# Odd attention: both heads' turned probabilities copied by one ScalarE operation, VectorE's copy removed

## The reference, cut to what matters

```python
def safe_softmax(s, mask):
    ...
    e = jnp.exp(s - m)
    den = jnp.sum(e, axis=-1, keepdims=True)
    return e / jnp.where(den > 0, den, 1.0)

def nsa_mixer(q, kc_raw, vc_raw, ks, vs, kw, vw, gates, pe, w1, w2, pos):
    ...
        p_cmp = safe_softmax(s, (cmp_end[None, :] <= t[:, None])[:, None, None, :])
        o_cmp = jnp.einsum('bqghn,bngd->bqghd', p_cmp.astype(v_cmp.dtype), v_cmp)
        ...
        o_slc = jnp.einsum('bqghnl,bgqnld->bqghd', p.astype(vg.dtype), vg)
        ...
        o_win = jnp.einsum('bqghs,bsgd->bqghd', p.astype(vwb.dtype), vwb)
        g = qslice(gates, i, C_Q_BLOCK)
        return g[..., 0:1] * o_cmp + g[..., 1:2] * o_slc + g[..., 2:3] * o_win
```

## Time and profile before

| | us |
|---|---|
| median of three runs | 1133.84 |
| the profiled execution, whole | 1134.03 |
| its span | 1132.3 |
| PE busy | 998.5 |
| DVE busy | 590.4 |
| ACT busy | 486.2 |
| POOL busy | 101.8 |

### The profile page before, as it was taken

One profiled execution on the slowest core, in us unless ns is written; L12 is line 12 of the kernel. 1 busy time (PEld: TensorE's weight loads), 2 busy tenths in 40 slices (PEclk: granted clock), 3 DMA queues, 4 the chain that ended last, 5 costly groups with the idle time before them and its releaser, 6 DMA issues. The chain is left out here.

```text
span 1132.3 us, 20170 instructions
## 1 busy us (share of the span) xinstructions
PE 998.5 (88%) x8499; PEld 713.1 (63%) x8499; DVE 590.4 (52%) x950; ACT 486.2 (43%) x795; POOL 101.8 (9%) x111
## 2 busy tenths in 40 slices
PE   6998899889666677998889999997998879999996
PEld 5676787445333344886537777775985546777773
DVE  5666678431000004688675554536666865655543
ACT  5455463310000004554556455524545656645532
POOL 3410270000000001034000000002040000000000
PEclk9998799889888899998889999998998999999998
DMA  8823004999999996452094755534421056666520
GB/s 275 253 82 120 2 3 173 424 408 419 420 421 421 421 413 215 150 181 80 1 312 136 250 184 184 197 111 147 155 82 75 1 186 205 223 222 207 186 88 37
DMA packets 108324, 228.56 MB, mean 202 GB/s; under 512 B 7145, under 2 KB 86043, under 8 KB 93659
## 3 DMA queue, kind: packets, MB, share of 16 engines
q1 hardware_dynamic: 105275, 219.38, 53.3%
q0 software_dynamic: 2976, 8.14, 2.4%
HBM read 224.63 MB, written 1.05 MB: 199 GB/s over the span
## 5 line engine op out<-in xcount | busy, mean ns | idle before, releaser
L524 DVE SCALAR_TENSOR_TENSOR ffn_wu_lo<-ffn_w_up,ffn_wu_hi 128x2048 f16<-128x2048 f32 x44 | 99.0, 2288 | 55.2 <-ACT ffn_wu_hi L449 55.2
L1132 PE MATMUL rw_pB<-ring,kept 128*32 128x256 f32 x864 | 72.6, 434 | 26.9 <-DMA ring<-in_w_up 22.5
L669 PE MATMUL ffn_pG<-ffn_hT_hi,ffn_wu_hi 128*128 128x256 f16 x352 | 95.9, 273 | 0.3
L669 PE MATMUL ffn_pU<-ffn_hT_hi,ffn_wu_hi 128*128 128x256 f16 x352 | 96.0, 273 | 0.0
L669 PE MATMUL ffn_pU<-ffn_hT_lo,ffn_wu_hi 128*128 128x256 f16 x352 | 96.0, 273 | 0.0
L669 PE MATMUL ffn_pU<-ffn_hT_hi,ffn_wu_lo 128*128 128x256 f16 x352 | 96.0, 273 | 0.0
L669 PE MATMUL ffn_pG<-ffn_hT_hi,ffn_wu_lo 128*128 128x256 f16 x352 | 95.9, 273 | 0.0
L669 PE MATMUL ffn_pG<-ffn_hT_lo,ffn_wu_hi 128*128 128x256 f16 x352 | 95.9, 273 | 0.0
L449 ACT ACTIVATE ffn_wu_hi<-ffn_w_up 128x2048 f16<-128x2048 f32 x44 | 81.7, 1901 | 2.4 <-DMA ffn_w_up<-in_ffn_w_gate 2.3
L1132 PEld LDWEIGHTS rw_pB<-ring,kept 128*32 128x32 f32 x864 | 39.1, 125 | 53.4 <-issue 40.7
L1065 DVE TENSOR_TENSOR rw_mu_a<-rw_pB,rw_mu_a 128x256 f32<-128x256 f32 x8 | 3.4, 425 | 130.6 <-PE rw_pB L1132 130.6
(11 more groups left out here) (655 smaller groups left out, 2141.0 us busy)
## 6 DMA issues: line engine op xcount, KB each, us to landing
ring<-in_w_gate SPq DMA_DIRECT2D x27, 1024.0 KB, 26.4
ring<-in_w_up SPq DMA_DIRECT2D x27, 1024.0 KB, 26.5
ring<-in_w_down SPq DMA_DIRECT2D x24, 1024.0 KB, 26.3
ffn_w_up<-in_ffn_w_gate SPq DMA_DIRECT2D x22, 1024.0 KB, 7.7
ffn_w_up<-in_ffn_w_up SPq DMA_DIRECT2D x22, 1024.0 KB, 9.9
ffn_w_down<-in_ffn_w_down SPq DMA_DIRECT2D x22, 1024.0 KB, 5.1
wt<-in_ev_w_in SPq DMA_DIRECT2D x9, 1024.0 KB, 5.6
wt<-in_od_w_in SPq DMA_DIRECT2D x9, 1024.0 KB, 5.5
```

Of the source, the lines that this page charges most:

```text
L524: return nc.vector.scalar_tensor_tensor(out, whole, scale, hi, ALU.mult, ALU.subtract)
L669: ins = T.matmul(p[:, s, j * SEQ:(j + 1) * SEQ], w[:, s, m, c, j::NJ], h[:, c, :], start=(n == 0), stop=(n == 3 * KC - 1))
L1132: ins = nc.tensor.matmul(into[i * CAP:(i + 1) * CAP, 0:D_EXPERT], h[:, c, i * CAP:(i + 1) * CAP], held[:, c * D_EXPERT:(c + 1) * D_EXPERT] ...
```

## The change

ScalarE's `right(u)` becomes `copy_turned(u)`, at the same place of its order: it copies both banks of `pT` (2 times 384 columns) to both heads' part of `ET` in one operation. VectorE's `left(u)` goes. One semaphore, `probs_copied`, takes the place of `probs_left` and `probs_right`; TensorE waits for it where it waited for both. The even layer's attention, which has such copies of its own, stays as it is.

```diff
@@ ScalarE
-                    def right(u):
+                    def copy_turned(u):
                         act.wait_ge(probs_turned, u + 1)
                         if u >= 2:
                             act.wait_ge(summed, u - 1)
-                        nc.scalar.activation(ET[:, u % 2, 1, :], pT[:, 1, 0:NCOL], ACT.Copy).then_inc(probs_right, 1)
+                        nc.scalar.activation(ET[:, u % 2, :, :], pT[:, :, 0:NCOL], ACT.Copy).then_inc(probs_copied, 1)
...
-                        right(u)
+                        copy_turned(u)
@@ VectorE
-                    def left(u):
-                        dve.wait_ge(probs_turned, u + 1)
-                        if u >= 2:
-                            dve.wait_ge(summed, u - 1)
-                        nc.vector.tensor_copy(ET[:, u % 2, 0, :], pT[:, 0, 0:NCOL]).then_inc(probs_left, 1)
...
-                        left(u)
@@ TensorE, turn(u)
-                            pe.wait_ge(probs_left, u)
-                            pe.wait_ge(probs_right, u)
+                            pe.wait_ge(probs_copied, u)
@@ TensorE, add_values(u)
-                        pe.wait_ge(probs_left, u + 1)
-                        pe.wait_ge(probs_right, u + 1)
+                        pe.wait_ge(probs_copied, u + 1)
```

More of the change, by code:

```diff
@@ L3454, in sparse_attention @@
         with Stage(nc, "nsa", ["scored", "least", "exped", "weighed", "probs_turned",
-                               "probs_left", "probs_right", "summed", "high_out", "low_out", "c_scored", "c_masked",
+                               "probs_copied", "summed", "high_out", "low_out", "c_scored", "c_masked",
                                "c_less", "c_exped", "c_weighed", "c_turned", "c_out", "gate_exps", "vlink"]) as sems:
-            (scored, least, exped, weighed, probs_turned, probs_left, probs_right, summed,
+            (scored, least, exped, weighed, probs_turned, probs_copied, summed,
              high_out, low_out, c_scored, c_masked, c_less, c_exped, c_weighed, c_turned, c_out, gate_exps, vlink) = sems
```

## The result

The changed kernel takes 1137.65 us (median of 20 runs, 1131.99 to 1141.64), the kernel before 1133.88 in the 20 runs beside it (1127.4 to 1139.32): ratio 1.0031, 95% interval 1.0016 to 1.0046, so 1.8 to 5.2 us slower. Two later series of 12 runs gave 1.0023 (0.9992 to 1.0053) and 1.0041 (1.0017 to 1.0065). The ratios compare undisturbed executions only and need not equal the quotient of the medians. The forecast was 1137.0, a ratio of 1.0026 to the profiled execution of before.

A forecast was written before the change was run, and what follows sets the result against it. The attention's pace, set by a loop once through ScalarE and over TensorE (6.89 us per two units), was to pass to one through ScalarE twice (7.26). 0.45 + 1.90 + 0.31 + 0.36 = +3.0 on 1134.0: 1137.0 us, range 1134.8 to 1139.4.

The forecast's parts named there:

- The ScalarE copy: ScalarE's 16 copies grow from 384 to 768 columns, 0.808 us against 0.504, so +0.31 us each.
- The rings: Steady attention: the loop through ScalarE twice, 6.64 us, becomes 7.26 and sets the pace of two units.
- ring B: Steady attention: loop once through ScalarE, then over TensorE; sets today's pace, 6.89 us per two units, and becomes 7.20.
- The start: From the attention's first copies through the compressed scores to exps(5): +0.45 us.
- copy(13): Attention's tail: this copy makes turn(14) 0.31 us later still.
- The last values: Attention's end: copy(15) runs 0.81 us, TensorE follows 0.16 behind its end; +0.36 us.
- VectorE as the bound: Rival, odd steps: VectorE's copy delays its minimum, so removing it gains 3.3 us, 1130.7; chance 0.05.
- all hidden: Rival: ScalarE's 16.2 us of waits in the attention swallow the longer copies, 1134.0; chance 0.06.
- The dearer copy: Rival: +0.50 us a copy on some 14 copies on the path, +2.8 on top, 1139.8; chance 0.08.
- Ring B alone: Rival: turn does not hold exps in the steady attention, two units in 7.20 us, total 1136.7; chance 0.14.
- The clock: Rival behind the attention: TensorE's clock falls once more or not at all, 1138.7 or 1135.3; chance 0.07 each way.
- Two of the signs: Expected in the profile: exps named as waiting for turn, and the attention ending near 921.0 instead of 917.95.

The follow-up runs named there:

- three halves of E: Changed kernel with three halves of buffer E instead of two, so exps(u + 2) waits for turn(u - 1); one execution took 1136.57 us.
- the kernel with two: Changed kernel with ScalarE's one copy of 768 columns made as two of 384; one execution took 1134.94 us.
- filler: Changed kernel with ten products more on TensorE ahead of turn(14), scores computed again and never read; ratio 1.0023 (0.9999 to 1.0047).
- two copies ahead of exps: Kernel before, one copy on each engine, with ScalarE's copy moved ahead of exps(u + 2); ratios 0.9972 and 0.9979.

## Why the prediction was right, step by step

The time, 1137.65, lies in the range, and the sum, 3.0 us, in the interval of 1.8 to 5.2. That the median comes within 0.7 of 1137.0 is in part luck: two terms were sized too high, and the clock, which the sum left out, added to it where it fell, in two profiles of three. By its own steps:

- The shift of the block behind the attention: right. From the first issue of the next stage to the end of the span it is 213.46 us before and 213.43 after.
- VectorE's copy worth nothing in the steady stretch: right (6.88 with and without it). VectorE's subtraction starts 0.42 behind the high copy, as forecast (880.84 to 881.26).
- The ScalarE copy: 0.82 us in place, against 0.81 taken from the other stage's row, which has the same shape but is a Relu with a scale; whether that makes the difference was not tried. By the rule of the Trainium skill ("ScalarE: Activation LUTs", section "What ACT_TABLE_LOAD costs") it would have been 0.826; the 16 copies' mean is 0.824, so here the trace agrees with the page more closely than with the row I used.
- The rings: right. 7.26 was forecast, 7.27 measured, in all three profiles of the changed kernel; ring B at 7.20 is shown by three halves of E. The five periods from exps(5) to exps(15) went from 34.41 to 36.35 (871.97 to 908.32): +1.94, forecast +1.90.
- The start: mis-sized. copy(0) put turn(1) 0.31 later, in the sum and in the trace (copy to turn is 0.65 before, 0.96 after); from there to exps(5) the sum had +0.14 more (0.45 in all), and the trace has 0.11 less, so 0.20 in all. I took 0.81 from turn(2) to the transposes, a step from values behind turn, where they follow in 0.68; and of the 1.53 behind them 0.15 went, where I had allowed 0.03. Before, VectorE's copy L3578 had to stand behind its minimum L3513 and started 0.80 behind the transposes (870.97); now it starts 0.64 behind them (867.64). The kernel without VectorE's copy gives this term alone: 0.43 less from turn(1) to turn(3). With the 0.32 that copy(1) puts on turn(2) it makes the 0.11 less of the trace.
- copy(13): +0.31, forecast 0.31.
- The last values: mis-sized a little. In the second profile of the changed kernel, at the full clock, turn(15) to L3628 is 2.47 us (920.97 to 923.44), before 2.23: +0.24 instead of +0.36. The weights of the last eight products load 0.05 behind the copy's end, where I had 0.16 to PE.

Together 0.20 + 1.94 + 0.31 + 0.24 = +2.7 us of the change's own, 0.24%. The three series give 0.31, 0.23 and 0.41%, all with intervals that hold it. If the clock's fall came in the tail in two of three executions, as in the profiles, it would add 0.9 and the sum would be 3.6; that is an estimate from three profiles and not shown.

The rivals: VectorE as the bound and all hidden are excluded by the profile of the kernel without its copy and by 7.27. The dearer copy is excluded by 0.82 us for the copy and by 7.27, and a dearer one has its own number, 7.39, in the kernel with two; its price in the prediction was added wrongly, as 14 times 0.19 is 2.7 and not 2.8. Ring B alone is excluded by 7.27 against 7.20.

The clock is the rival that I priced in the wrong place. Its case was a fall more or less at the start of the next stage. There the fall came before and after alike (0.50 from 922 to 924 us in both), and that stretch is equally long. The fall that the change was followed by lay in the tail of the attention, in two profiles of three, where I had argued against it with the wait of 2.02 us, and it cost 1.3 instead of 1.7. A chance of 0.07 was small for that, though three profiles don't tell how often it comes. If in addition the low level at the start belonged to the changed kernel, the sum would be 2.7 + 3.1 = 5.8, an estimate that lies above the first interval.

Two of the signs did not show. Exps was not named as waiting for turn; that turn held it is shown by the distance of 0.08 and by three halves of E. And the attention's end cannot be held against 921.0: the next stage's first issue came at 919.57, 0.7 later than before and not 3.0, because the stage had begun 6.6 earlier.

## What to carry to other kernels

Close the rings before you price a merged operation: an engine with idle time can still be the one whose every microsecond counts, if its operation stands between two of the busiest engine. Two engines' copies side by side cost 0.50 where one engine's double copy costs 0.82, so here merging them lost while the copy stood on the ring and, by the profiles alone, gained once the order had taken it off. And look at the order first: putting the operation that frees the next step ahead of the long one that does not left the kernel some 5 us under the kernel before with one copy (and so some 8 under the changed kernel) and some 3 with two, and with it the one copy looks the better, where without it it was the worse.

## What the runs showed that I had not expected

- The name of a wait for two engines can be wrong: exps was put down to VectorE's minimum in each period, before and after. In every other step of the changed kernel that minimum had ended 0.40 us before exps, and turn 0.08 before; and cutting turn's link changed the pace. Compare the ends of all that an instruction waits for.
- TensorE's clock can fall inside a stage: behind a wait of 2.12 us (2.19 with two copies on ScalarE, 2.33 with three halves) it was at 0.50 in three of five profiles without filler, and cost 1.3 to 1.5 us; behind 2.01 or 2.02 us it stayed at 1.00 in three of three. The numbers are too few to call the difference a rule, and in the first profile with two copies ahead of exps it fell at 866 us with no wait longer than 1.07 us in the 5 us before.
- Two profiles of kernels with the same program ahead of a stage reached it 6.6 us apart (852.56 and 845.99). A difference of two spans says little of a change of 3 us; the same steady stretch in both timelines says it to 0.01.
